# A position-bias line stored once and spread by one DRAM-to-DRAM transfer, in place of 128 stored copies, in a two-layer hybrid attention step

## What is computed

```python
def t5_bucket(rel):                      # rel = key_pos - query_pos
    half = NUM_BUCKETS // 2
    max_exact = half // 2
    n = jnp.abs(rel)
    nf = jnp.maximum(n, 1).astype(jnp.float32)
    large = max_exact + (jnp.log(nf / max_exact) / math.log(MAX_DISTANCE / max_exact)
                         * (half - max_exact)).astype(jnp.int32)
    large = jnp.minimum(large, half - 1)
    return jnp.where(rel > 0, half, 0) + jnp.where(n < max_exact, n, large)

s = jnp.einsum("bqhmd,bkhmd->bhmqk", qb, k).astype(jnp.float32) * scale
bias = jnp.transpose(bias_table[t5_bucket(k_pos[None, :] - pos[:, None])], (2, 0, 1))
s = s + bias.astype(jnp.float32)[None, :, None]
```

## Time and profile before

| | before |
|---|---|
| time, median of 3 runs | 3345.43 us (3332.53 to 3347.3) |
| span of the profiled execution | 3352.0 us |
| TensorE matmuls, busy | 2952.4 us (88%), 17444 matmuls |
| VectorE, busy | 1472.2 us (44%) |
| ScalarE, busy | 935.4 us (28%) |
| GpSimd, busy | 252.4 us (8%) |
| moved by DMA | 200.52 MB, mean 60 GB/s |

### The profile page before, as it was taken

The page is one execution under the profiler, slowest core; times in us unless marked ns, Lnnn a source line. Parts: engine busy times, 40 slices in busy tenths (PEclk is TensorE's granted clock), DMA queues, the critical chain, the costliest instruction groups (busy, mean ns, idle before and its releaser), DMA issues.

```text
span 3352.0 us, 53277 instructions
## 1 busy us (share of the span) xinstructions
PE 2952.4 (88%) x17444; PEld 2686.8 (80%) x17444; DVE 1472.2 (44%) x2600; ACT 935.4 (28%) x2018; POOL 252.4 (8%) x694
## 2 busy tenths in 40 slices
PE   3588899977799989999979988998778998999996
PEld 3575589865499989999978656997457998999996
DVE  4364321124443467373756342112344335746465
ACT  2123223224422133221222231232443222312122
POOL 0210100110000011010101011000100000101010
PEclk7797689855599989999989786995558999999998
DMA  9530013420022222222223101233001222222221
GB/s 77 65 65 0 21 44 101 134 62 13 4 64 69 72 61 69 76 75 69 60 62 58 29 1 39 81 111 117 20 10 35 75 69 61 75 69 75 69 68 63
DMA packets 375511, 200.52 MB, mean 60 GB/s; under 512 B 65906, under 2 KB 367588, under 8 KB 375380
## 3 DMA queue, kind: packets, MB, share of 16 engines
q1 hardware_dynamic: 344642, 177.94, 19.0%
q0 software_dynamic: 3712, 7.90, 3.3%
q10 hardware_dynamic: 27026, 13.08, 1.3%
HBM read 180.50 MB, written 18.37 MB: 59 GB/s over the span
## 4 chain that ended last, share of the span: by engine, by line
PE 74%; DVE 8%; ACT 6%; issue 6%; DVEq 3%; another core or an unknown queue 2%; ACTq 1%; DMA 1%; POOL 0%; SPq 0%; POOLq 0%
PE acc L489 19%; PE acc L493 19%; PE acc L490 19%; PE tq L849 1%; ACT d_s L1040 1%; DVE d_s L1479 1%; PE tq L590 1%; PE tp L818 1%; PE tq L747 1%; DVE rstd L1429 1%; DVEq L1480 1%; PE acc L528 1%; PE acc L562 1%; PE acc L531 1%
## 5 line engine op out<-in xcount | busy, mean ns | idle before, releaser
L489 PE MATMUL acc<-hn_hi,w_hi 128*128 128x328 f32 x2848 | 879.4, 315 | 58.4 <-DVE w_lo L1411 58.4
L490 PE MATMUL acc<-hn_lo,w_hi 128*128 128x328 f32 x2848 | 876.0, 313 | 0.0
L493 PE MATMUL acc<-hn_hi,w_lo 128*128 128x328 f32 x2848 | 661.9, 314 | 0.0
L1411 DVE TENSOR_TENSOR w_lo<-w_raw,w_hi 128x1024 fp32r<-128x1024 f32 x298 | 364.5, 1223 | 673.8 <-ACT w_hi L1000 671.2
L489 PEld LDWEIGHTS acc<-hn_hi,w_hi 128*128 128x128 f32 x2848 | 537.5, 189 | 60.3 <-issue 60.1
L1000 ACT ACTIVATE w_hi<-w_raw 128x1024 fp32r<-128x1024 f32 x298 | 315.1, 1059 | 919.0 <-PE acc L493 652.7
L490 PEld LDWEIGHTS acc<-hn_lo,w_hi 128*128 128x128 f32 x2848 | 537.9, 189 | 0.2
L493 PEld LDWEIGHTS acc<-hn_hi,w_lo 128*128 128x128 f32 x2848 | 484.4, 189 | 0.0
L489 PE MATMUL acc<-s_hi,w_hi 128*128 128x328 f32 x704 | 221.2, 320 | 18.6 <-DVE w_lo L1411 14.1
L490 PE MATMUL acc<-s_lo,w_hi 128*128 128x328 f32 x704 | 220.7, 319 | 0.0
L493 PE MATMUL acc<-s_hi,w_lo 128*128 128x328 f32 x704 | 167.2, 320 | 0.0
(11 more groups left out here) (317 smaller groups left out, 4634.4 us busy)
## 6 DMA issues: line engine op xcount, KB each, us to landing
w_raw<-in_w_in SPq DMA_DIRECT2D x96, 512.0 KB
w_raw<-in_w_up SPq DMA_DIRECT2D x88, 512.0 KB
w_raw<-in_w_down SPq DMA_DIRECT2D x32, 512.0 KB
out<-tok_out ACTq DMA_DIRECT2D x32, 256.0 KB, 2.3
k_past<-in_cache_a_k SPq DMA_DIRECT2D x16, 512.0 KB, 4.2
v_past<-in_cache_a_v SPq DMA_DIRECT2D x16, 512.0 KB, 3.5
w_raw<-in_w_a_br SPq DMA_DIRECT2D x16, 512.0 KB
w_raw<-in_w_out SPq DMA_DIRECT2D x16, 512.0 KB
```

The lines of the kernel that those rows point to most:

```text
L489: mm(acc[:, slot, c, 0:HALF], w_hi[:, slot, k, :], x_hi[:, k, cols], start=(k == 0), stop=False)
L490: mm(acc[:, slot, c, 0:HALF], w_hi[:, slot, k, :], x_lo[:, k, cols], start=False, stop=False)
L493: last = mm(acc[:, slot, c, 0:HALF], w_lo[:, slot, k, :], x_hi[:, k, cols], start=False, stop=(k == nk - 1))
L1411: tt(w_lo[:, slot], w_raw[:, slot], w_hi[:, slot].bitcast(F32), ALU.subtract).then_inc(w_split[slot], 1)
```

## The change

The line is stored once per head, by one transfer of 8 rows, into a DRAM tensor of 8 x 655. A second transfer, from DRAM to DRAM, reads each line 128 times, each time one element earlier, and writes a table of 8 planes of 128 rows of 528 values. GpSimd waits for the first transfer, and then for the second (`lines_spread`), before the 48 small loads. These and the 16 loads of `d_bias` now read the finished table, at a row pitch of 2112 bytes. The two waits of ScalarE and VectorE now ask for one transfer.

```diff
-        line_dram = nc.dram_tensor("bias_line_dram", (H, P, REL), F32, kind="Internal").ap()
-        toeplitz = bass.AP(line_dram.tensor, P - 1, [[P * REL, H], [REL - 1, P], [1, PM]])
+        line_dram = nc.dram_tensor("bias_line_dram", (H, REL), F32, kind="Internal").ap()
+        lines = bass.AP(line_dram.tensor, P - 1, [[REL, H], [-1, P], [1, PM]])
+        toeplitz = nc.dram_tensor("toeplitz", (H, P, PM), F32, kind="Internal").ap()
...
-                e.wait_ge(line_stored, 16 * H)
+                e.wait_ge(line_stored, 16)
...
             e.wait_ge(line_ready, 1)
-            for h in range(H):
-                e.dma_start(line_dram[h:h + 1], bias_line[h:h + 1, :].rearrange("h (o n) -> h o n", o=1).to_broadcast([1, P, REL])).then_inc(line_stored, 16)
-            e.wait_ge(line_stored, 16 * H)
+            e.dma_start(line_dram, bias_line[:]).then_inc(line_stored, 16)
+            e.wait_ge(line_stored, 16)
+            e.dma_start(toeplitz, lines).then_inc(lines_spread, 16)
+            e.wait_ge(lines_spread, 16)
             for h in range(H):
                 for m in range(2):
                     row = 32 * (h % 4) + 16 * m
                     for col, n, rel in ((0, PAST, -PAST), (PAST, META, -PAST - META), (PAST + META, DEC, 0)):
-                        src = bass.AP(line_dram.tensor, h * P * REL + rel - REL0, [[REL - 1, DEC], [1, n]])
-                        e.dma_start(sbias[row:row + DEC, h // 4, col:col + n], src).then_inc(sbias_loaded, 16)
+                        first = rel - REL0 - (P - 1)
+                        e.dma_start(sbias[row:row + DEC, h // 4, col:col + n], toeplitz[h, 0:DEC, first:first + n]).then_inc(sbias_loaded, 16)
```

More of the change, by code:

```diff
@@ L251, in build @@
         past_wait = sem("past_wait")
-        consts_loaded, x_turned, h_updates, line_ready, line_stored, sbias_loaded, ones_set = (
+        consts_loaded, x_turned, h_updates, line_ready, line_stored, lines_spread, sbias_loaded, ones_set = (
             sem(n) for n in ("consts_loaded", "x_turned", "h_updates", "line_ready", "line_stored",
-                             "sbias_loaded", "ones_set"))
+                             "lines_spread", "sbias_loaded", "ones_set"))
         par_loaded, par_turned, par_ready, lam_summed, lam_exped, layer_start = (
```

## The result

| | before | after |
|---|---|---|
| time, median | 3342.9 us (4 runs, 3332.5 to 3347.3) | 3291.45 us (4 runs, 3281.4 to 3297.7) |
| ratio | | 0.9838, 95% interval 0.9813 to 0.9863 |
| span of the profiled execution | 3352.0 us | 3279.7 us |

The ratio is a gain of 54 us, with an interval from 46 to 63, clear of no change; the two medians differ by 51.5 us. The forecast was 3289.4 us and a gain of 56.

A forecast was written before the change was run, and what follows sets the result against it. The bias-line stores were taken to block the weights on TensorE's path. 54.5 us of stall plus 1.5 of clock make 56.0, so the median 3345.4 becomes 3289.4 us; range 3272 to 3308.

The forecast's parts named there:

- The stall and its cause: GpSimd's eight bias-line stores block block 2's weights; without them `w_hi` moves from 115.83 to about 61.3 us, gaining 54.5 us.
- The clock: TensorE, at half speed after the idle stretch, keeps its clock up with the shorter pause: 1.5 us gained, bounds 0 and 1.6.
- The store: GpSimd's one transfer of 8 rows, 21 KB, issued at 16.2 us, lands at about 19.3; bounds 2 to 5 us.
- The spread: New DRAM-to-DRAM transfer of 2.16 MB: 12 us, starting at 19.5, ending at 31.5; price zero if over by 57.
- Eight engines: Rival: spread dealt out by planes to eight engines, taking 48 us; gain 44.3 us, time 3301 us; chance 0.10.
- As slow as the stores: Rival: re-reading one line is slow in DRAM too; spread takes 77 us, gain 15.3, time 3330 us; chance 0.07.
- slower than before: Rival: 8 engines at 1.8 GB/s each, spread 154 us, TensorE resumes 62 us later, time 3407 us; chance 0.03.
- The rows cut into elements: Rival: the spread's backward-stepping rows are cut into 4-byte elements, 980 us, time over 4200; chance 0.02.
- The 48 small loads: GpSimd's `sbias` loads run from 31.8 to about 55 us, with 64 us of cover before the rotary key; price 0.
- The 16 planes: `d_bias` loads at the new pitch: two waits, 10.3 us together, can gain at most 3.6 us or lose about as much; taken as 0.
- the sign of being wrong: The forecast would be wrong if, among other signs, the planes of `d_bias` landed later than 4.6 us.
- Nothing comes back later: After `kbT` every stage lies 56 us earlier; the 55 us gained do not return as idle TensorE later.

The follow-up runs named there:

- four and six heads: Kernel before, with 4 or 6 heads stored the old way (128 reads of one partition) and the rest copied in DRAM: 3299.94 and 3316.99 us, one run each.
- second profile of the change: The changed kernel run again unaltered, against the kernel before: 3291.92 us against 3347.39, ratio 0.983.

## Why the prediction was right, step by step

- *The stall and its cause.* The 54.7 us at one wait were read as the stores' doing, and the term was 54.5; measured 54.44. That the stores and nothing else caused it is shown by the source alone being exchanged (61.61 us), and by four and six heads giving 73.61 and 95.39.
- *The clock.* 1.5 us taken, with 1.6 as its bound; between `w_hi` and `kbT` the lead grew from 54.44 to 56.12, so 1.7. The granted clock of 1.00 from 58 to 80 us bears it out.
- *The store* was put at 3 us and took 2.0.
- *The spread* was put at 12 us, between 8.7 and 24, and took 14.4. It cost nothing, as said, because it was over at 33 us with 57 as the latest. That the size came near is luck, by a compensation. I priced it at 16.4 GB/s for one engine on 16 engines. It ran on 8, at 1.82 MB in 0.507 x 16 x 10 = 81 engine-us, so 22 GB/s each.
- *Eight engines* was a rival with 0.10, and half of it came true: the spread is dealt out by planes to 8 engines. By the rule that the prediction set beside this rival the spread gets 8 engines, and so it did; the chance was too low for that half. Its price was what failed: 48 us doubled an upper bound of eight planes landing one after another. At the planes' own rate half of the engines need 16.5 us, as the prediction says in the same place, and 14.4 were measured.
- *As slow as the stores* and *slower than before* are excluded: the spread took 14.4 us, not 77 or 154.
- *The rows cut into elements* did not occur: 14.4 us.
- *The 48 small loads* ended at 56.2 us and GpSimd then waited 62.9 us (64 predicted). Cost zero, as said.
- *The 16 planes* were taken as zero within 3.6 us. The two waits went from 10.3 to 8.7 us, but with the old slanted table they are anything from 8.8 to 10.9 in the experiments, and 9.9 in the second profile of the change. No effect of the table is to be seen in that scatter. The planes land in 3.2 us at the most after the change, so the sign of being wrong, above 4.6, did not show.
- *Nothing comes back later.* From 163 us of the span to 1890 the lead stays between 53 and 63 us, moving both ways. In the stretch of the 437 matmuls it was the granted clock that moved it; for the smaller steps that is only likely.
- *The last 2 us.* That the median came within 2.1 us of the forecast is partly luck: the runs of one kernel lie up to 16 us apart in that comparison, and the interval of the gain reaches from 46 to 63 us. The span of the profiled execution was forecast at 3296.0 us and was 3279.7. The firm part is the 54.44 and 56.12 us at the two points of the trace.

One reading in the prediction was stronger than its row. I wrote that the stores blocked the weights, from a stretch without a packet of SyncE's queue. That they are held to the very end of the stores is now shown by the 1.9 us in the experiments with four and six heads. Why a queue gets next to no turn beside these slow packets stays open; the run from ScalarE's queue shows only that it is not peculiar to GpSimd's.

## What to carry to other kernels

When DMA engines are busy and move a tenth of what they can (30 GB/s from 80 to 100 us here, where from 9 to 16 us they moved 313), look for the transfer whose packets are long in time, and then for what its source or destination has in common: here eight stores, each of which reads one partition of SBUF 128 times. Half of the engines held in this way are enough to hold a load that is spread over all. A transfer that nobody waits for can still be on the critical path, through the loads that stand behind it. Copies of a small line are made in DRAM, from one stored copy, rather than out of SBUF; if they must come out of SBUF, source partitions 4 apart were 3.4 times as fast as adjacent ones, for eight partitions from 0 on.

## What was not expected of the hardware

- SBUF read by DMA from one partition gave 27.5 GB/s in all, with 16 engines asking. Eight partitions give 48, 88 or 165 GB/s, as they are 0 to 7, 16 apart, or 4 apart.
- DRAM to DRAM, 8 engines carried 21 to 22 GB/s each and 16 only 15 each, with the rows in another order: 17.4 and 13.9 us for 2.68 MB.
- A transfer that held 8 of 16 engines held a weight block as surely as one that held all: 0.52 MB of two blocks' 1.05 landed, and `w_hi` waited 11.70 us, until the transfer's end.
- A queue that is backed up holds the engine that issues: eight issues from ScalarE took 71.56 us, with the same stores that GpSimd issued in 4.29.
- The same 437 matmuls took 101 us in one execution and 108 in another of one kernel, at a granted clock of 0.85 and 0.77, with the other engines' busy time within 0.4 us.
